# Moving the late modulation sums of a transformer block from the attention units to the units after the delta heads

## What is computed

```python
cond = jax.nn.silu(c)
ada = cond @ w_ada[layer] + b_ada[layer]            # 2048 x 12288 weights, 100 MB
shift_m, scale_m, gate_m, shift_f, scale_f, gate_f = split(ada, 6)
h = rmsnorm(x, norm_pre_mix) * (1 + scale_m) + shift_m
y = token_mixer(h, ...)                             # attention, delta rule, gates, output products
x = x + gate_m * rmsnorm(y, norm_post_mix)
h = rmsnorm(x, norm_pre_ffn) * (1 + scale_f) + shift_f
x = x + gate_f * rmsnorm(peer_ffn(h, ...), norm_post_ffn)
```

## Time and profile before

| | |
|---|---|
| median of 3 runs | 5450.12 us (5445.65 to 5451.69) |
| the profiled execution | 5450.39 us, its span 5448.6 us |
| mean granted TensorE clock | 0.974 of full speed |
| busy: PE, DVE, ACT, POOL | 95%, 49%, 26%, 54% of the span |
| matmul weight loads busy | 81% |
| memory traffic | 154 GB/s over the span |

### The profile page before, as it was taken

One profiled execution on the slowest core, in us unless ns is written; L12 is line 12 of the kernel. 1 busy time (PEld: TensorE's weight loads), 2 busy tenths in 40 slices (PEclk: granted clock), 3 DMA queues, 4 the chain that ended last, 5 costly groups with the idle time before them and its releaser, 6 DMA issues.

```text
span 5448.6 us, 67159 instructions
## 1 busy us (share of the span) xinstructions
PE 5150.4 (95%) x25699; PEld 4407.2 (81%) x25699; DVE 2664.6 (49%) x4370; ACT 1428.1 (26%) x2021; POOL 2936.9 (54%) x1124
## 2 busy tenths in 40 slices
PE   2878899999999999999899999999999899999997
PEld 1566678788888888787678888888888799999997
DVE  6777730344444443034477656662000057666764
ACT  1100110133333332100232233333222233333332
POOL 1445557644444444777534433344444488888873
PEclk6989999999999999999999999999999999999999
DMA  7455422321221121233233344344333489898983
GB/s 311 166 181 182 170 105 93 124 70 63 68 69 66 62 69 66 92 119 120 96 114 110 112 137 149 137 148 152 121 119 121 133 283 315 315 316 316 318 315 142
DMA packets 245042, 839.93 MB, mean 154 GB/s; under 512 B 24080, under 2 KB 89744, under 8 KB 200624
## 3 DMA queue, kind: packets, MB, share of 16 engines
q1 hardware_dynamic: 127632, 562.09, 29.8%
q10 hardware_dynamic: 94752, 141.98, 7.7%
q0 software_dynamic: 22528, 134.30, 6.4%
HBM read 766.91 MB, written 71.37 MB: 154 GB/s over the span
## 4 chain that ended last, share of the span: by engine, by line
PE 79%; DVE 10%; DMA 5%; issue 3%; ACT 1%; POOL 0%; ACTq 0%; SPq 0%; DVEq 0%
PE bank L835 9%; PE bank L837 9%; PE bank L839 9%; PE bank L518 8%; PE bank L522 8%; PE bank L520 8%; PE bank L932 6%; PE bank L934 6%; PE bank L933 6%; DVE hacc L1548 4%; DMA half<-ada_late 3%; PE bank L898 2%; PE bank L732 2%; PE wide L743 2%; DMA raw<-stream 1%
## 5 line engine op out<-in xcount | busy, mean ns | idle before, releaser
L460 POOL TENSOR_TENSOR lo<-raw,hi 128x1024 fp32r<-128x1024 f32 x528 | 1278.0, 2422 | 1145.4 <-ACT hi L1237 1141.7
L444 POOL TENSOR_TENSOR hi<-raw,ones 128x2048 fp32r<-128x2048 f32 x168 | 612.2, 3644 | 1240.0 <-PE bank L522 985.5
L518 PE MATMUL bank<-xh,hi 128*128 128x512 f32 x2624 | 1105.1, 421 | 42.4 <-POOL lo L447 13.6
L522 PE MATMUL bank<-xh,lo 128*128 128x512 f32 x2624 | 1035.3, 395 | 0.0
L520 PE MATMUL bank<-xl,hi 128*128 128x512 f32 x2624 | 1034.8, 394 | 0.0
L1237 ACT ACTIVATE hi<-raw 128x1024 fp32r<-128x1024 f32 x528 | 547.4, 1057 | 1221.2 <-PE bank L839 1043.3
L835 PE MATMUL bank<-xh,hi 128*128 128x512 f32 x2176 | 858.8, 395 | 8.9 <-DVE xl L1478 8.9
L837 PE MATMUL bank<-xl,hi 128*128 128x512 f32 x2176 | 848.1, 390 | 0.0
L839 PE MATMUL bank<-xh,lo 128*128 128x512 f32 x2176 | 847.9, 390 | 0.0
L447 POOL TENSOR_TENSOR lo<-raw,hi 128x2048 fp32r<-128x2048 f32 x168 | 801.6, 4772 | 13.2
L932 PE MATMUL bank<-CH,hi 128*128 128x384 f32 x2048 | 694.2, 339 | 14.0 <-DVE R L1934 9.8
(11 more groups left out here) (276 smaller groups left out, 5810.9 us busy)
## 6 DMA issues: line engine op xcount, KB each, us to landing
raw<-stream SPq DMA_DIRECT2D x528, 512.0 KB, 3.9
raw<-stream SPq DMA_DIRECT2D x184, 1024.0 KB, 4.8
half<-ada_late SPq DMA_DIRECT2D x128, 512.0 KB, 4.0
act_d<-etile ACTq DMA_DIRECT2D x128, 256.0 KB, 2.0
G_d<-stage ACTq DMA_DIRECT2D x12, 2048.0 KB, 7.5
Gt<-G_d ACTq DMA_DIRECT2D x32, 768.0 KB, 14.6
cf<-act_d ACTq DMA_DIRECT2D x31, 768.0 KB, 17.6
arow<-stream SPq DMA_DIRECT2D x16, 1024.0 KB, 7.3
```

Of the source, the lines that this page charges most:

```text
L444: nc.gpsimd.tensor_tensor(hi[slot][:, :], raw[s][:, :], ones[:, 0:1].to_broadcast([P, D]), ALU.mult).then_inc(hi_done, 1)
L460: nc.gpsimd.tensor_tensor(lo_h[slot], raw_h[h % 4], hi_h[slot].bitcast(F32), ALU.subtract).then_inc(f_lo[h % 4], 1)
L518: nc.tensor.matmul(out, hi[slot][:, w], at_k(xh, k), start=(k == 0), stop=False, skip_group_check=True)
L522: mm = nc.tensor.matmul(out, lo[slot][:, w], at_k(xh, k), start=False, stop=(k == KT - 1), skip_group_check=True)
```

## The change

- The 128 halves leave the attention units. SP loads them beside the weights of units GD 8 to MIX 15: four with each of ten units, then three with each of sixteen, then three with each of thirteen and one more. Units are counted by the load they go with; DVE works off the first 40 as they come, in GD, then three behind each unit of WDO and of MIX (the first 13), and the last one.
- `hacc` is now PSUM: banks 4 and 5, and 6 and 7. There are four `half` buffers for the first 88 halves and two for the rest. A half's transfer starts only when the one two before has landed.
- ACT copies each finished accumulator to `hsum` in SBUF (`keep_late`), PE sums over the partitions in k-step 8 of GD 10 and 14, WDO 4, 9 and 14, MIX 4, 10 and 15. `turn_v` no longer waits for the bias.
- The gains of the later norms (L1463) are made behind MIX. GD, WDO and MIX are written out on PE, GD on ACT and WDO on DVE, where hardware loops stood.

```diff
-        half = [place(f"half{s}", [P, D // 2], F32, tail + s * D * 2) for s in range(2)]
-        hacc = [place(f"hacc{s}", [P, D // 2], F32, (r2 + 14 * T * 4, tail + 5 * T * 4)[s]) for s in range(2)]
+        half = [place(f"half{s}", [P, D // 2], F32, (offset["acst"], tail)[s // 2] + s % 2 * D * 2) for s in range(4)]
+        hacc = [wide[:, s * (D // 2):(s + 1) * (D // 2)] for s in range(2)]
+        hsum = place("hsum", [P, D // 2], F32, tail + 4 * T * 4)
...
-        sums_at = range(5, 5 + HALVES // 4, 4)
+        late_gd, late_wdo, late_mix = [4] * 10, [3] * 16, [3] * 13 + [1]
+        n_mix = sum(late_gd) + sum(late_wdo)
+        turned_gd, turned_wdo, turned_mix = {10: 0, 14: 1}, {4: 2, 9: 3, 14: 4}, {4: 5, 10: 6, 15: 7}
...
+        def late_slot(n):
+            return half[n % 2 if n >= n_mix else n % 4][:, :]
...
+            def load_half(n):
+                if n >= 2:
+                    sp.wait_ge(half_full[n % 2], n // 2 * 16)
+                if n >= n_mix:
+                    sp.wait_ge(half_used[n % 2], n // 2)
+                elif n >= 4:
+                    sp.wait_ge(half_used[n % 2], n // 2 - 1)
+                sp.dma_start(late_slot(n), ada_late[n, :, :]).then_inc(half_full[n % 2], 16)
...
-            sp.wait_ge(s_h, KT)
-            with sp.Fori(0, HALVES // 8) as i:
-                for s in range(2):
-                    for j in range(4):
-                        if j == 2:
-                            load(i + (ADA_USES + 1), s)
-                        load_half(i * 8 + (s * 4 + j), i * 4 + (s * 2 + j // 2), j % 2)
-            with sp.Fori(ADA_USES + 1 + HALVES // 8, uses) as i:
+            first = B_GD // 2 + 4
+            with sp.Fori(ADA_USES + 1, ADA_USES + first) as i:
                 for s in range(2):
                     load(i, s)
+            sp.wait_ge(d_done, NH + ONE)
+            n = 0
+            late = late_gd + late_wdo + late_mix
+            for i in range(first, MIX_USES):
+                for s in range(2):
+                    load(ADA_USES + i, s)
+                    for _ in range(late.pop(0) if late else 0):
+                        load_half(n)
+                        n += 1
+            while n < HALVES:
+                load_half(n)
+                n += 1
...
-            turned = [0]
-            summed = [2]
-                pe.wait_ge(half_used[1], (q + 1) * (KT // 2) + ONE)
-                if turned[0]:
-                    pe.wait_ge(s_vtc, turned[0])
+                pe.wait_ge(s_hs, q + 1)
+                pe.wait_ge(s_ada, 2 + q)
                 for n in range(KT // 2):
-                    mm = nc.tensor.matmul(bank[3][:, n:n + 1], hacc[q % 2][:, n * P:(n + 1) * P], ones[:, 0:1],
+                    mm = nc.tensor.matmul(bank[3][:, n:n + 1], hsum[:, n * P:(n + 1) * P], ones[:, 0:1],
-                summed[0] += 1
+            def late_between(at, unit):
+                return (lambda k: sum_late(at[unit]) if k == 8 else None) if unit in at else None
...
-                pe.wait_ge(s_ada, summed[0])
-                turned[0] += 1
...
+            for u in range(4, U_GD):
+                product(u % 2, (B_GD + u) // 2, bank[u % 2][:, :], late_between(turned_gd, u))
+            for base, split, at in ((B_WDO, s_ol, turned_wdo), (B_MIX, s_ml, turned_mix)):
+                for u in range(KT):
+                    product(u % 2, (base + u) // 2, bank[u % 2][:, :], late_between(at, u),
+                            ready=None if u else (split, 0))
...
+            def keep_late(q):
+                for s in range(2):
+                    act.wait_ge(half_used[s], (q + 1) * (KT // 2))
+                if q:
+                    act.wait_ge(s_adamm, 2 + q + ONE)
+                nc.scalar.activation(hsum[:, :], hacc[q % 2], ACT.Copy).then_inc(s_hs, 1)
+            for u in range(4, U_GD):
+                dgate(u // 2, u % 2)
+                if u + 1 in turned_gd:
+                    keep_late(turned_gd[u + 1])
...
+            for q in turned_wdo.values():
+                keep_late(q)
...
+                if k + 1 in turned_mix:
+                    keep_late(turned_mix[k + 1])
...
+            def late_half(n):
+                q, k, s = n // KT, n % KT, n % 2
+                dve.wait_ge(half_full[s], (n // 2 + 1) * 16)
+                if k == 0:
+                    if q >= 2:
+                        dve.wait_ge(s_hs, q - 1)
+                    v.tensor_scalar(hacc[q % 2], late_slot(n), cond[:, 0:1], None, ALU.mult).then_inc(half_used[s], 1)
+                else:
+                    dve.wait_ge(half_used[1 - s], (n - 1) // 2 + 1)
+                    v.scalar_tensor_tensor(hacc[q % 2], late_slot(n), cond[:, k:k + 1], hacc[q % 2],
+                                           ALU.mult, ALU.add).then_inc(half_used[s], 1)
+            def late_ada(q):
+                c = slice((4 + q) * KT // 2, (5 + q) * KT // 2)
+                dve.wait_ge(s_adamm, 3 + q + ONE)
+                v.tensor_tensor(ada[:, c], bank[3][:, 0:KT // 2], vec[:, c], ALU.add).then_inc(s_ada, 1)
...
+            n_late = 0
+            for n in late_gd:
+                for _ in range(n):
+                    late_half(n_late)
+                    n_late += 1
+                if n_late == 36:
+                    late_ada(0)
...
+            late_ada(1)
+            for u in range(U_WDO):
+                s = u % 2
+                dve.wait_ge(unit_done[s], (B_WDO + u) // 2 + 1 + ONE)
+                x, g = row_k(R1, u), row_k(R2, u)
+                v.scalar_tensor_tensor(g, g, 1.0, bank[s][:, :], ALU.add, ALU.mult).then_inc(bank_free[s], 1)
+                dve.wait_ge(bank_free[s], (B_WDO + u) // 2 + 1)
+                v.tensor_tensor(x, x, g, ALU.add).then_inc(s_mrg, 1)
+                for _ in range(late_wdo[u]):
+                    late_half(n_late)
+                    n_late += 1
+                if u - 1 in turned_wdo:
+                    late_ada(turned_wdo[u - 1])
...
+                for _ in range(late_mix[k] if k < len(late_mix) else 0):
+                    late_half(n_late)
+                    n_late += 1
+                if k - 1 in turned_mix:
+                    late_ada(turned_mix[k - 1])
+            dve.wait_ge(s_ada, 2 + HALVES // KT)
+            for n, m in ((1, GATE_M), (2, SCALE_F), (3, GATE_F)):
+                gains(n, m)
+            step.sync()
```

More of the change, by code:

```diff
@@ L808, in _ @@
                 product(j % 2, B_GD // 2 + j // 2, bank[j % 2][:, :], lambda k, j=j: delta_steps(NH - 1, 1, j, k))
-            with pe.Fori(2, U_GD // 2) as i:
-                for s in range(2):
-                    product(s, i + B_GD // 2, bank[s][:, :])
-            for base, split in ((B_WDO, s_ol), (B_MIX, s_ml)):
-                for s in range(2):
-                    product(s, base // 2, bank[s][:, :], ready=None if s else (split, 0))
-                with pe.Fori(1, KT // 2) as i:
-                    for s in range(2):
-                        product(s, i + base // 2, bank[s][:, :])
+            for u in range(4, U_GD):
[4 more added lines that the diff above has]
+                            ready=None if u else (split, 0))
             pe.wait_ge(s_ss, 2 * KT)
@@ L1426, in _ @@
             v = nc.vector
[L1428 removed]
+            ahead = (d_done, d_sso, d_rso, q_s, s_adamm, *unit_done, *arow_used)
             for n, x in enumerate(ahead):
@@ L1568, in _ @@
                         rotate(h, a - 1)
-                    late_halves(4 * u + 2)
-            dve.wait_ge(s_ada, 2 + HALVES // KT)
-            for n, m in ((1, GATE_M), (2, SCALE_F), (3, GATE_F)):
-                gains(n, m)
             for i in range(4):
```

41 lines of the change are left out of this document (6 added, 35 removed).

## The result

The changed kernel takes 5329.09 us in the median of 4 runs (5322.13 to 5338.29), the kernel before, run beside it, 5450.9 (4 runs, 5445.65 to 5451.87). The ratio is 0.978, with a 95% interval of 0.9765 to 0.9795: 2.2% faster. The forecast was 5318 and the range 5300 to 5338. The profiled execution is the slowest of the four, 5338.29 us with a span of 5336.4, so it shows some 9 us more than the median; this has a cause that the text comes to.

What follows compares the result with a forecast made beforehand. PE was taken to be held up in attention by late DVE work and split weights, then slow clock. 5450.4 − 150.6 (attention) + 14.7 (sums) + 2.4 (GD 14) + 1.0 (edges, small terms) = 5317.9, say 5318 us; range 5300 to 5338.

Steps and rivals of the forecast that it cites:

- rival 2: GD 8 to 15 and both edges: new waits at sums and edges add 8 to 20 us, 5326 to 5338; chance 0.11.
- What bounded the kernel: Attention, 160 to 780 us: PE idle 98.5 us, waiting for DVE's work and split weights, then matmuls at half clock.
- What the attention units give back: Attention units without waits: heads 1 to 3 gain 120.3 us, head 0's units 2 to 8 21.6; whole sum −150.6.
- rival 1: Attention: the clock gives back all its 56 us, gain 169 instead of 150.6 us, so 5299; chance 0.04.
- Unit 1: Attention, head 0: 10.88 + 1.20 + about 0.9 = 13.0 us against 21.7, gain 8.7.
- GD 14: K-step 8 there: PE's second sum waits for the first bias, made after half 36; +2.4 us, ends 0.9 and 5.7.
- Sums, additions, copies, loads: GD, WDO and MIX: PE's late sums add 14.7 us at 1.84 each; additions, copies and transfers hidden, 0.
- Rival 3: Attention: PE keeps waiting for probabilities or weights, half of 57.2 us with the clock behind it: +35, 5353; chance 0.05.
- Rival 4: WDO and MIX: POOL blocks DVE's additions; 5513 at 4.1 us each, slower than before from 3.6; chance 0.02.

Runs made afterwards that it cites:

- the second profile: The changed kernel run once more, unedited: 5323.49 us (5322.95 to 5323.91, 4 runs), ratio 0.9774.

## Why the prediction was right, and where its terms were off

The forecast of 5318 us was met within some 11 us (5329.09) and 6 us (5323.49). The direction, the place of the gain and its size are no luck: they follow from the terms below. That the first median lies in the range is in part luck: it is above the forecast's own upper end of 5325, in the part that was added for rival 2, whose mechanism was not what happened.

- **What bounded the kernel.** Right. The waits for probabilities, bias and weights in attention went with the halves, and the clock came back with them. That it was not the order of DVE's list alone is shown: putting the mask first changes nothing (1.0). That DVE's additions and POOL block each other over SBUF is shown at the new place, where putting the accumulators back costs 96 us; for the attention units it is argued from the same long additions, and the halves' late arrival has a share there that no run separates.
- **What the attention units give back.** The terms for heads 1 to 3 (120.3 us) and for units 2 to 8 of head 0 (21.6) came out to 0.1 us: a unit's length built from 10.88, 1.20, 0.49 and the small work of head 3 holds for all three heads, and rival 1, which takes the clock's 56 us whole, was wrong by the overlap that the prediction named. With nothing late left the kernel takes 5302.0; without the sums and the wait in GD 14 this rival would be 5281.9 (5299 − 14.7 − 2.4), the forecast 5300.8. The Trainium skill (TensorE: Matmul & The Clock Gate, Terms) has that penalty rule; the measured units speak for the smaller 37 us here. The trace before shows the overlap itself: added up in stretches of 1 us from 160 to 780, the share of the clock that was missing comes to 54.6 us of all time, but to 34.3 us of the time in which PE was busy; the other 20 us were idle and are in the waits already.
- **Unit 1** is the step that failed: "10.88 + 1.20 + about 0.9 = 13.0", a gain of 8.7. Without any wait it takes 170.88 − 156.38 = 14.5, so the 0.9 for its small work was 1.5 too little. The larger part is a wait that the step left out. The earlier trace rows had 4.5 us for a row operation, and it was booked as part of the gain; in its place the first profile has 1.8 and 7.3 us, with slow matmuls behind the longer one, and the second 1.7 with slow matmuls behind it (the clock was 0.62 from 168 to 172 in the version with the earlier bias, whose wait is the same 1.7). Units 1 and 2 lost 38.5 − 25.7 = 12.8 us in the first profile and 30.6 − 25.7 = 4.9 in the second. The question not asked was what the halves had covered: with them gone from DVE's list, row operations with SBUF inputs moved 7.6 us forward, under POOL's split.
- **GD 14.** The one new wait was found, at its place and with its cause, but mis-sized: 2.4 us with ends of 0.9 and 5.7 stand against 20.6 − 12.7 = 7.9 in the second profile or 21.9 − 12.7 = 9.3 in the first. Two things were short. The pairs were given 4.0 us each from the earlier trace rows and 1.5 for the `raw` beside them, 9.5 with the `raw`'s issue as the start; they took 11.7, and a half 5.6 in the median. The median of the earlier trace rows is from attention units and from GD before the change, where at most two halves and a `raw` are wanted at a time; here five transfers follow one another. And the wait was booked without the clock behind it: 4.59 us idle, then about 10 us at half clock, which by the difference cost some 3.4 (7.9 − 4.5) to 4.7 us (9.3 − 4.6) more.
- **Sums, additions, copies, loads.** Sums in WDO and MIX: 11.6 measured, 12.0 given. Additions 1.29, given 1.28. Units of GD, WDO and MIX without a sum stay at 10.88. Rival 2 was partly true in its result (its 5326 to 5338 holds the first measurement's 5329, not the second's 5323). Of its mechanism only the late halves at one sum, in GD 14, took place: no half held PE in WDO or MIX, and POOL's idle time for weights there, 20.3 us, cost PE nothing. Rival 3 had no share; the waits for the probabilities are none. Rival 4 is real as a mechanism and was ruled out rightly by the place in PSUM. The Trainium skill (SBUF — State Buffer, Who interferes with whom) says that a DVE instruction with at most one SBUF input stays out of GpSimd's way, outside the modes that use both of DVE's ports, and that one with two SBUF inputs contends with GpSimd's reads; the prediction gave the rule without that exception. The additions agree (1.29 against 3.06 us). So does L1517: with its one input and its output in SBUF it is blocked for 4.41 us, from PSUM it is not (0.68), which fits the exception for the two-port modes, since it takes 0.42 when free.
- **The total.** 5318 plus 12.8 and 6.7 is 5337.5, beside 5338.3 profiled. In the second profile the same two places give +4.9 and +5.3, and unit 0, WDO with MIX and the part behind them were 4.2 us shorter in sum than in the forecast, which leaves 5323.9.

What stays open: the two outcomes in unit 1 were seen in profiles only, the longer in two and the shorter in four with the same lists, so how often each comes is not known, nor why the clock falls behind the same wait in some executions. The wait of PE for L1980 in the feed-forward part (5.6 to 11.8 us over the profiles, also in the kernel before) was not studied.

## What to carry to other kernels

When work leaves an engine's list, ask two things: what waited for it, and what it stood in front of. The second moves forward, and may land under another engine's instruction that blocks it; an edit at the blocked operation only hands the block to the next one, while placing the other engine's long instructions in the gaps removes it. When a new wait's size depends on transfers, price them from a stretch where the queue is as full as it will be, and add the slow clock that follows PE's idle time.

## What the runs showed of the hardware that had not been expected

- One-input operations can be blocked too: `tensor_scalar` from SBUF to SBUF on 16 x 512 took 0.42 us free and 4.41 under POOL's split; from PSUM 0.68 under it. A second one (L1525) took 0.48 free and 3.71 under a split. The four scans took 1.36 free, 5.58 and 9.04 with both inputs in SBUF under a split, and 1.37 with one input in PSUM under one.
- PE idle for 4.6 us in GD 14 was followed by some 10 us at 1.2 GHz in the first profile (granted clock 0.50 to 0.51), so that the stall cost about twice its length.
- The same wait of PE, 1.7 to 1.8 us in unit 1, was followed by a clock of 1.00 in two profiles and by a few us at 0.50 in four; the executions that kept the clock were the longer ones in these two units, 38.5 us against 30.6.
- Freeing PE can cost time: with its waits put later, POOL's split, released by PE, came sooner and blocked DVE's row operations longer, and units 1 and 2 took 36.1 us against 30.6.
